# A diffusion backbone in fp32 on one core: the head of the kernel put into another order

## What is computed

```python
for i in range(2):
    m = split(silu(c) @ w_mod[i] + b_mod[i], 9)          # 9 vectors of 1024
    h = h + 0.5 * m[2] * swiglu(modulate(rms_norm(h), m[0], m[1]), w_ff_in[i, 0], w_ff_out[i, 0])
    a = modulate(rms_norm(h), m[3], m[4])
    y = fourier_mix(a, ...) if i == 0 else conformer_conv(a, ...)
    h = h + m[5] * y
    h = h + 0.5 * m[8] * swiglu(modulate(rms_norm(h), m[6], m[7]), w_ff_in[i, 1], w_ff_out[i, 1])

def rms_norm(x):         return x * rsqrt(mean(x * x, axis=-1) + 1e-6)
def modulate(h, b, s):   return h * (1 + s) + b
def swiglu(h, wi, wo):   g, u = split(h @ wi, 2); return (silu(g) * u) @ wo     # 1024 -> 2 * 2816 -> 1024
```

## Time and profile before

| | before |
|---|---|
| median of 3 runs (lowest, highest) | 1856.62 us (1856.01, 1858.68) |
| the profiled execution | 1856.64 us, span 1854.9 us |
| TensorE busy | 1803.0 us (97%) |
| VectorE busy | 1197.2 us (65%) |
| ScalarE busy | 619.6 us (33%) |
| DMA | 238.10 MB, mean 128 GB/s |

### The profile page before, as it was taken

One profiled execution on the slowest core, in us unless ns is written; L12 is line 12 of the kernel. 1 busy time (PEld: TensorE's weight loads), 2 busy tenths in 40 slices (PEclk: granted clock), 3 DMA queues, 4 the chain that ended last, 5 costly groups with the idle time before them and its releaser, 6 DMA issues.

```text
span 1854.9 us, 22066 instructions
## 1 busy us (share of the span) xinstructions
PE 1803.0 (97%) x8604; PEld 1485.3 (80%) x8604; DVE 1197.2 (65%) x1541; ACT 619.6 (33%) x796; POOL 170.1 (9%) x148
## 2 busy tenths in 40 slices
PE   5899999998999999999999999999999999999999
PEld 2688888888798888888988888889764898888888
DVE  6866767567767675676776766547798555444454
ACT  2532222235342222222432222225766542222221
POOL 0000000002110000000200000002995200000000
PEclk8999999998999999999999999999999999999999
DMA  8853634431436344363253453421120322413201
GB/s 293 272 187 115 219 119 163 176 113 47 136 114 218 123 161 179 113 217 123 69 200 140 144 195 113 136 68 46 46 92 24 116 89 69 136 68 112 91 23 69
DMA packets 160395, 238.10 MB, mean 128 GB/s; under 512 B 3805, under 2 KB 110509, under 8 KB 160204
## 3 DMA queue, kind: packets, MB, share of 16 engines
q1 hardware_dynamic: 160016, 236.99, 36.9%
q10 hardware_dynamic: 316, 0.23, 0.0%
HBM read 235.11 MB, written 2.10 MB: 128 GB/s over the span
## 4 chain that ended last, share of the span: by engine, by line
PE 85%; DVE 5%; POOL 4%; ACT 3%; DMA 1%; issue 1%; SPq 0%; POOLq 0%; DVEq 0%; ACTq 0%
PE bank L1670 16%; PE bank L1677 15%; PE bank L1672 15%; PE bank L1545 10%; PE bank L1547 10%; PE bank L1546 10%; POOL tmp_c L628 3%; PE bank L1927 2%; PE bank L1615 1%; DVE mod_acc L1025 1%; PE bank L1617 1%; PE bank L1619 1%; DVE w_lo L992 1%; DMA raw_pair<-in_w_mod 1%; POOL sq_sum L593 1%
## 5 line engine op out<-in xcount | busy, mean ns | idle before, releaser
L1670 PE MATMUL bank<-a_hi,w_hi 128*128 128x512 f32 x1408 | 552.6, 392 | 6.2 <-ACT a_hi L686 4.7
L1672 PE MATMUL bank<-a_hi,w_lo 128*128 128x512 f32 x1408 | 549.3, 390 | 0.0
L1677 PE MATMUL bank<-a_lo,w_hi 128*128 128x512 f32 x1408 | 434.8, 390 | 1.7 <-DVE a_lo L1100 1.6
L1670 PEld LDWEIGHTS bank<-a_hi,w_hi 128*128 128x128 f32 x1408 | 265.3, 188 | 63.7 <-issue 6.3
L1218 DVE SCALAR_TENSOR_TENSOR h<-bank,half_gate,h 128x512 f32<-128x512 f32 x320 | 233.5, 746 | 122.3 <-PE bank L1547 121.7
L1677 PEld LDWEIGHTS bank<-a_lo,w_hi 128*128 128x128 f32 x1408 | 264.8, 188 | 57.7 <-DVE a_lo L1100 2.7
L1672 PEld LDWEIGHTS bank<-a_hi,w_lo 128*128 128x128 f32 x1408 | 265.4, 188 | 56.3 <-issue 1.4
L1545 PE MATMUL bank<-p_hi,w_hi 128*128 128x512 f32 (+1 forms) x768 | 287.6, 375 | 1.1 <-DVE h L1225 0.6
L1547 PE MATMUL bank<-p_lo,w_hi 128*128 128x512 f32 (+1 forms) x768 | 285.9, 372 | 0.0
L1546 PE MATMUL bank<-p_hi,w_lo 128*128 128x512 f32 (+1 forms) x768 | 285.7, 372 | 0.0
L992 DVE TENSOR_TENSOR w_lo<-raw_pair,w_hi 128x2048 fp32r<-128x2048 f32 x102 | 235.4, 2308 | 51.8 <-ACT w_hi L800 47.9
(11 more groups left out here) (197 smaller groups left out, 1851.6 us busy)
## 6 DMA issues: line engine op xcount, KB each, us to landing
raw_pair<-in_w_ff_in SPq DMA_DIRECT2D x88, 1024.0 KB, 7.4
raw_mod<-in_w_mod SPq DMA_DIRECT2D x66, 1024.0 KB, 8.3
raw_down<-in_w_ff_out SPq DMA_DIRECT2D x44, 1024.0 KB, 8.6
raw_pair<-in_conv_w_in SPq DMA_DIRECT2D x8, 1024.0 KB, 6.6
raw_pair<-in_w_mod SPq DMA_DIRECT2D x6, 1024.0 KB, 15.2
raw_pair<-in_fnet_w_out SPq DMA_DIRECT2D x4, 1024.0 KB, 6.2
raw_pair<-in_conv_w_out SPq DMA_DIRECT2D x4, 1024.0 KB, 6.6
raw_mod<-in_x SPq DMA_DIRECT2D x4, 512.0 KB, 5.0
```

The costliest lines, as they stand in the source:

```text
L1670: pe.matmul(ps[banks + s][:], tile_hi, a_hi[:, k], start=k == 0, stop=False, skip_group_check=True)
L1672: pe.matmul(ps[banks + s][:], tile_lo, a_hi[:, k], start=False, stop=False, skip_group_check=True)
L1677: ins = pe.matmul(ps[banks + s][:], w_hi[b][:, s * KD + k], a_lo[:, k], start=False, stop=k == KD - 1, skip_group_check=True)
```

## The change

It touches the head up to the end of the first two `up` products. Most other lines of the diff only shift semaphore counts or swap the two slots of `raw_pair`.

- **x by token tile.** Each of the 4 loads of x has a semaphore of its own; TensorE turns a tile as it lands, 4 channel chunks per PSUM bank, and VectorE copies 4 chunks of 128 tokens at once.
- **Squares.** ScalarE squares the 8 chunks once h is complete; TensorE sums them with a 128x128 matrix of 1/1024 in fp32 (8 matmuls of 128x512), so that the mean stands on all partitions. ScalarE takes the root of 128x512, VectorE its reciprocal in place (128x512). The adds on VectorE, `token_sums` and the first `spread_rstd` go.
- **Buffers and loads.** x goes to slot 0, unit 0 to slot 1, unit 2 to `raw_mod`; after `head_mac(0)` the first weight pair to slot 1, then unit 3 to slot 0; after `head_sum` of unit 2, unit 1 to `raw_mod`; after that of unit 3, the second pair to slot 0; after `head_mac(1)`, unit 4 to `raw_mod`.
- **Halves.** Chunks 0 to 3 of the norm need only units 0 and 2. Their columns are made first (`head_transpose(0)`, `head_columns(0)`), the four chunks are normed, and TensorE starts the first two `up` products over these channels. `head_mac(1)`, the columns of units 1 and 3 and chunks 4 to 7 come after.

```diff
-            sp.wait_ge(s_h, KD)
-            head_load(3)
             sp.wait_ge(s_mod_mac, KD)
-            head_load(1)
-            sp.wait_ge(s_head_sum, 1)
-            ff_pair(0, 0, 0)
-            sp.wait_ge(s_head_sum, 2)
-            (unit 4 to raw_mod)
-            sp.wait_ge(s_mod_mac, 2 * KD)
-            ff_pair(0, 1, 1)
+            ff_pair(0, 0, PAIR[FFA])
+            sp.wait_ge(s_h, KD)
+            head_load(3)
+            sp.wait_ge(s_head_sum, 1)
+            head_load(1)
+            sp.wait_ge(s_head_sum, 2)
+            ff_pair(0, 1, PAIR[FFA] + 1)
+            sp.wait_ge(s_mod_mac, 2 * KD)
+            (unit 4 to raw_mod)
...
+            def x_squares():                                   # ScalarE
+                act.activation(table_dummy[:], eps_col[:], ACT.Sqrt)
+                act.wait_ge(s_h, KD)
+                for o in range(KD):
+                    if o >= 2:
+                        act.wait_ge(s_x_sum, o - 1)
+                    act.activation(tmp_a[:, o % 2], h[:, o], ACT.Square).then_inc(s_sq, 1)
+                act.wait_ge(s_x_sum, KD)
+                act.activation(sq_sum[:], ps[RSTD_BANK][:], ACT.Sqrt, bias=eps_col[:], scale=1.0)
...
+            x_squares()
+            mod_hi(0)
+            pair_hi(FIRST[FFA][0], PAIR[FFA], 0)
+            pair_hi(FIRST[FFA][1], PAIR[FFA], 1)
+            act.wait_ge(s_mod, 2)
+            head_chunks(range(4))
+            mod_hi(1)
+            act.wait_ge(s_mod, 4)
+            head_chunks(range(4, KD))
...
             head_mac(0)                                        # VectorE
             mod_lo(0)
-            mod_row(0)
-            token_rstd(0)
-            head_row(2)
-            head_mac(1)
-            mod_lo(1)
-            head_row(3)
-            mod_row(1)
+            x_rstd()                                           # reciprocal of sq_sum, 128x512
             (copies of the vectors)
-            pair_lo(FIRST[FFA][0], 0, 0)
-            mod_columns(0)
-            normed(0, h, [(4, lambda: pair_lo(FIRST[FFA][1], 0, 1))])
+            pair_lo(FIRST[FFA][0], PAIR[FFA], 0)
+            mod_row(0)
+            head_row(2)
+            head_columns(0)
+            normed(0, h, range(4), [(1, lambda: pair_lo(FIRST[FFA][1], PAIR[FFA], 1))])
+            head_mac(1)
+            mod_lo(1)
+            head_row(3)
+            mod_row(1)
+            head_columns(1)
+            normed(0, h, range(4, KD))
...
-            head_sum(2)                                        # TensorE
-            mod_sum(0)
-            token_sums(0)
+            for o in range(KD):
+                pe.wait_ge(s_sq, o + 1)
+                pe.matmul(ps[RSTD_BANK][:], mean_w[:], tmp_a[:, o % 2], start=o == 0, stop=o == KD - 1)
             (vectors turned)
-            spread_rstd(0)
-            head_sum(3)
-            mod_sum(1)
-            mod_transpose(0)
+            head_half(2, 0)
+            mod_sum(0)
+            head_half(2, 1)
+            head_transpose(0)
+            head_half(3, 0)
...
+            def head_up():
+                for half in range(2):
+                    for ch, (b, use) in enumerate(UP[0]):
+                        for k in range(4 * half, 4 * half + 4):
+                            (wait for chunk k; 6 matmuls)
+                            if ch == 0 and k == 3:
+                                head_half(3, 1)
+                            if ch == 1 and k == 1:
+                                mod_sum(1)
+                            if ch == 1 and k == 3:
+                                head_transpose(1)
```

More of the change, by code:

```diff
@@ L292, in hybrid_backbone @@
         s_vec_in = sem("vec_loaded")
-        s_x_in = sem("x_loaded")
+        s_x_in = [sem(f"x_tile{t}_loaded") for t in range(TC)]
+        s_x_sum = sem("x_square_summed")
         s_head_in = [sem(f"head_half_loaded{n}") for n in range(2 * HEAD)]
@@ L660, in mod_hi, with modulated @@
                 act.activation(mod_acc_hi[:], mod_acc[:], ACT.Copy).then_inc(s_mod_hi, 1)
-            def squares(n, src, after=()):
-                q = n // 5
[L664 to L684, removed]
+            def x_squares():
[6 more added lines that the diff above has]
+                act.wait_ge(s_x_sum, KD)
+                act.activation(sq_sum[:], ps[RSTD_BANK][:], ACT.Sqrt, bias=eps_col[:], scale=1.0).then_inc(s_std, 1)
+            def modulated(n, func, scale, bias, ks=range(KD)):
+                q = n // 5
+                for k in ks:
                     act.wait_ge(s_t, KD * q + k + 1)
@@ L796, in next_hi @@
                 pair = PAIR[FF_PHASE[f]] + par + 1
-                act.wait_ge(s_pair_in[pair % 2], (i - par) * 16 + 32 * (pair // 2 + 1))
+                act.wait_ge(s_pair_in[pair % 2], (i - par) * 16 + 32 * ((pair + 1) // 2))
                 b = UP[f][ch][0]
@@ L1093, in token_rstd, with normed @@
                                       ALU.mult).then_inc(s_diag, 1)
-            def normed(n, src, after=()):
+            def normed(n, src, ks=range(KD), after=()):
                 q = n // 5
@@ L1349, in add_mixer_bias @@
                 dve.wait_ge(s_bias, (KD + 1) * (layer + 1))
-            for d in range(KD):
-                dve.wait_ge(s_take, d + 1)
-                dve.tensor_copy(h[:, d], ps[d % 4][:]).then_inc(s_h, 1)
-                if d >= 1:
-                    square_add(0, d - 1)
-            square_add(0, KD - 1)
+            for e in range(KD):
+                t, half = e // 2, e % 2
+                dve.wait_ge(s_take, e + 1)
+                dve.tensor_copy(h[:, 4 * half:4 * half + 4, t * P:(t + 1) * P],
+                                ps[e % 4][:].rearrange("p (d n) -> p d n", d=4)).then_inc(s_h, 1)
             def head_mac(unit):
@@ L1565, in mod_transpose @@
                 ins.then_inc(s_mod_t, 1)
-            def head_sum(unit):
-                for half in range(2):
-                    pe.wait_ge(s_head_in[2 * unit + half], 16)
-                    for k in range(4 * half, 4 * half + 4):
-                        ins = pe.matmul(ps[HEAD_BANK[unit]][0:ROWS, :], silu_c[:, k:k + 1].to_broadcast([P, ROWS]),
-                                        head_rows[unit][:, k], start=k == 0, stop=k == KD - 1)
-                ins.then_inc(s_head_sum, 1)
-            def token_sums(n):
-                pe.wait_ge(s_sq_sum, ADDS * (n // 5 + 1))
-                for t in range(TC):
-                    ins = pe.matmul(ps[TOK_BANK][:, t:t + 1], sq_sum[:, t * P:(t + 1) * P], ones[:, 0:1],
-                                    start=True, stop=True, skip_group_check=True)
-                ins.then_inc(s_tok, 1)
@@ L1583, in spread_rstd, with head_half @@
-            def spread_rstd(n):
-                for t in range(TC):
-                    pe.wait_ge(s_diag, TC * (n // 5) + t + 1)
+            def head_half(unit, half):
+                pe.wait_ge(s_head_in[2 * unit + half], 16)
+                for k in range(4 * half, 4 * half + 4):
+                    ins = pe.matmul(ps[HEAD_BANK[unit]][0:ROWS, :], silu_c[:, k:k + 1].to_broadcast([P, ROWS]),
+                                    head_rows[unit][:, k], start=k == 0, stop=k == KD - 1, skip_group_check=True)
+                if half == 1:
+                    ins.then_inc(s_head_sum, 1)
```

134 lines of the change are left out of this document (73 added, 61 removed).

## The result

In comparison runs the kernel before took 1856.68 us (median of 15, 1855.53 to 1858.68) and the changed one 1861.52 us (median of 15, 1859.79 to 1864.12). The ratio is 1.0026, 95% interval 1.0019 to 1.0033: **4.8 us slower**. The forecast was 3.0 us slower. The profiled execution of the changed kernel took 1864.12 us (span 1862.3), which is its slowest of the 15 by 1.6 us.

The account below looks back on a forecast made before the run. The prediction took VectorE's start of `ring_mac(4)` to set the time until TensorE's full stretch from about 90 us. Its terms 1.8 + 0.6 + 0.6 gave 3.0 us later, 1859.6 us, range 1855.5 to 1863.

Parts of the forecast that it names:

- What bounds: Up to TensorE's restart near 90 us: the time follows VectorE's start of `ring_mac(4)`, not TensorE's first product.
- x and unit 0: Start of the head: unit 0's loads land at 15.8 and 20.4, `head_mac(0)` ends at 23.6, gain 2.3 us.
- Squares: TensorE's 8 fp32 sums in the head: end at 20.4, root at 21.1, hidden by 3.9 us.
- the rival: Half clock in the squares: sums take 13.7 us, to 26.8, costing 1.0 us, total 1860.6; chance 15%.
- Reciprocal: VectorE's 128x512 reciprocal in the head: 4.5 us, hidden by the first weight pair's load with 2.9 us to spare.
- First pair and first chunk: In the head: first weight pair lands at 31.8, `pair_hi` ends at 33.7, first chunk starts at 38.1 instead of 48.07.
- First product near 42: TensorE's first `up` product starts at about 42 instead of 49.8.
- Second columns: Columns for chunks 4 to 7: VectorE waits some 2 us for TensorE's transposes, ready at 58.8.
- the term of 1.8 us: End of VectorE's head: `ring_mac(4)` starts at 66.3 against 64.46, 1.8 us later.
- Loads: Queue behind the second pair's issue at 52.3: unit 5 lands at 77.1, VectorE waits 0 to 1 us, 0.6 taken.
- Clock: Behind TensorE's restart: more half clock after some 5 us idle in two pieces, 0.6 us more.
- the load queue: Rival on loads behind 52.3: 3.4 us per MB, VectorE waits 5.0 us for unit 5, total 1864.0; chance 10%.

Follow-up runs that it names:

- plain_pass: Changed kernel with a plain copy of 128x512 in place of the reciprocal of the root: 1861.49 us, ratio 1.0028.
- three_reciprocals: Changed kernel with the reciprocal made three times in a row: 1864.98 us, ratio 1.0044.
- busy_gap: Changed kernel with 20 matmuls of 128x128 in TensorE's idle time before `head_transpose(0)`: 1861.93 us, ratio 1.0026.
- warm_restart: Changed kernel with 9, 8 and 8 dummy matmuls of 128x128 ahead of TensorE's three waits before its restart: 1861.04 us, ratio 1.0022.
- unit5_first: Changed kernel with unit 5's loads issued ahead of the third weight pair and the first down weights: 1860.9 us, ratio 1.0021.
- transpose_early: Changed kernel with TensorE's `mod_sum(1)` one chunk and `head_transpose(1)` two chunks earlier among the products: ratio 1.0028.
- before_warm: Kernel before with 8 dummy matmuls of 128x128 in TensorE's 1.96 us gap before 90.07: 1857.15 us, ratio 0.9995.

## Why the prediction came out as it did

The direction and the mechanism held; the size was 1.8 us short. Its steps, against plain_pass and the changed kernel's own trace:

- **What bounds: right.** In plain_pass TensorE waited for VectorE three times between 73 and 94 (2.29, 3.48 and 2.15 us; forecast were two), and the lead turned to idle time.
- **x and unit 0: right.** Halves landed where the earlier trace rows put them (VectorE starts at 16.00 and 21.29 against 15.8 and 20.4), `head_mac(0)` ends 23.3 in plain_pass, 24.4 here; forecast 23.6.
- **Squares: right, and the rival fell.** The sums end at 19.6 (forecast 20.4). From 12 to 20 the clock was 1.00 in the changed kernel's trace. By the Trainium skill ("TensorE: Matmul & The Clock Gate", section "What's actually happening"), activity lifts the slow clock; the trace agrees here, with the transposes of x ahead of the squares.
- **Reciprocal: hidden, its price too high.** 3.35 us instead of 4.5. The Trainium skill's repeat count of 8 ("VectorE: DVE Perf Modes", section "First, the fixed hardware budget") had made some 5 us; measured are 3.35 / 0.64 = 5.2 of the prediction's plain passes, and the measurement decides. Behind the reciprocal there were 4.4 us to spare, not 2.9, and three_reciprocals used them up.
- **First pair and first chunk: right.** `pair_lo` at 33.48 in plain_pass (33.7 forecast), 34.55 here.
- **First product near 42: wrong**, 42.9 in plain_pass and 45.4 here. The step priced `head_half(3, 0)` at full clock, though TensorE stands idle 5 us ahead of it; busy_gap, with that gap filled, has 41.55. Without effect on the median (busy_gap), 1.3 to 1.5 us in the profiled execution of the changed kernel.
- **Second columns: right.** 58.91 in plain_pass, 58.8 forecast, wait 1.89 against 2. `ring_mac(4)` 66.29 against **66.3**: the term of 1.8 us is right to 0.03.
- **Loads: the step that failed, by size.** The term for VectorE's wait for unit 5 was 0.6 us; measured are 1.69 and 1.67, outside its 0 to 1. Unit 5 landed at 78.0 in plain_pass, 0.9 after the forecast 77.1, and the sum itself gave 0.85, of which 0.6 was taken. The pair's issue (52.3) was right. The loads of unit 4's first half and unit 5's first half, issued at 53.69 and 69.17, to landing:

```profile
raw_mod<-in_w_mod SPq DMA_DIRECT2D x1, 1024.0 KB, 10.3
raw_mod<-in_w_mod SPq DMA_DIRECT2D x1, 1024.0 KB, 8.9
```

Unit 4's first half, the third load after the pause in the queue, landed at 64.0 where the working has 52.3 + 5.2 + 2 × 2.8 = 63.1, so the 0.9 us are already there; the five loads from it to 78.0 took 2.8 each. In the trace's semaphore events the first load landed at 57.45, 5.2 after its issue as forecast, and the next two 3.1 and 3.5 us apart. The rate of 2.8 us per MB was thus too fast for these two; the third one's last part-completion came 0.8 us after the other fifteen. With this term VectorE's part to the restart is 1.8 us longer than before instead of 0.6.
- **Clock: the size met, the working not.** Forecast 0.6. From restart to landmark plain_pass needs 50.39 − 49.64 = 0.75 us more, the changed kernel 1.44. The sum took half of the half-clock time as cost; runs with a full clock show that some 0.8 us of it is hidden, as VectorE's next row is then the later one. And what it called 5 us of idle time in two pieces was 7.9 in three.

In sum for plain_pass: 1.83 + 1.79 + 0.75 = 4.4 us at the landmark, against 1.8 + 0.6 + 0.6 = 3.0; the medians say 4.8, and the last 0.4 us are not assigned. Of the rivals only the load queue's direction was seen, with a wait of 1.7 us instead of its 5.0; its mechanism, 3.4 us for every MB, was not.

The changed kernel's own trace has `ring_mac(4)` at 68.68 instead of 66.29, for two reasons. The first pair is 1.1 us later because unit 0's second half landed at 21.26 instead of 20.19, so that `head_mac(0)` ended and the pair was issued at 24.43 instead of 23.36. The rest is the longer half clock. The traces of warm_restart and unit5_first, whose head is the changed one's, have the longer half clock too (6.07 and 6.29 us for `head_half(3, 0)`) and `ring_mac(4)` at 68.2 and 67.8; transpose_early (5.23) and plain_pass (5.10) have the shorter one. No run settles what makes it long, or how often it is.

## What to carry to other kernels

Ask which engine's chain reaches the saturated stretch last, and count a change by what it does there: starting TensorE 4 to 7 us earlier was worth nothing, taking the 6 us of `head_mac(1)` off VectorE, together with a better order, was worth 5. Splitting a stage into halves inserts other work into that chain and puts small steps that others wait for behind big ones; lay the order of every small hand-over by hand, before measuring the idea. Where two limits stand within 2 us, as the chain and the load here, remove both in one trial, since here either alone showed nothing that the medians could tell.

## What the runs showed of the hardware

- VectorE's reciprocal of 128x512 fp32 takes 3.35 us, a plain copy 0.42.
- TensorE ran at half clock after idle times of 5.1 to 9.3 us in the head (5.10 to 6.43 us for eight records that took 3.62 when dummies filled the gap). At the restart it came back at half clock after idle times of 3.5 and 2.15 us with 0.6 us of work between (plain_pass). In the kernel before, after 1.96 us, it came back at full clock (90.07) and the clock fell to half at about 91.7, in the middle of work. Dummies of 128x128 in the gaps kept the clock at 1.00 behind them in all four kernels that had them.
- Identical work behind the head isn't identical in time. before_warm is 0.25 us ahead of before at 413, and 1.3 us behind at 677, in these pairs of rows:

```profile
412.93 0.75 DVE L1218 SCALAR_TENSOR_TENSOR h<-bank,half_gate,h 128x512 f32<-128x512 f32 x1 [0.61 <-PE bank L1547]
676.71 2.05 DVE L1218 SCALAR_TENSOR_TENSOR h<-bank,half_gate,h 128x512 f32<-128x512 f32 x3
...
412.68 0.75 DVE L1218 SCALAR_TENSOR_TENSOR h<-bank,half_gate,h 128x512 f32<-128x512 f32 x1 [0.61 <-PE bank L1547]
678.02 2.05 DVE L1218 SCALAR_TENSOR_TENSOR h<-bank,half_gate,h 128x512 f32<-128x512 f32 x3
```

At 140 and at 413 us the distance is the same to 0.01 us; behind that it changes, by 1.6 us in this pair and most in warm_restart, which is 4.3 us behind before at the landmark and 6.6 at the end of the span. Between single executions a landmark just behind the changed stretch therefore resolves tenths of a microsecond where the whole time resolves one or two.
